# Two feed-forward blocks on one Trainium2 core: gate and up products over two token thirds as seven block products instead of eight

## The reference, cut to what matters

```python
def swiglu_ffn(x, g, w_gate, w_up, w_down):
    h = rmsnorm(x, g)
    return (jax.nn.silu(h @ w_gate) * (h @ w_up)) @ w_down

x = x + 0.5 * swiglu_ffn(x, lp['ffn1_norm'], ...)
...                                    # attention, gated DeltaNet, cross-attention
x = x + 0.5 * swiglu_ffn(x, lp['ffn2_norm'], ...)
```

## Time and profile before

| | us |
|---|---|
| median of 3 runs | 3365.69 |
| the profiled execution, time | 3355.45 |
| its span, first to last instruction | 3353.7 |
| PE busy | 3228.4 (96%) |
| DVE / ACT / POOL busy | 1323.4 / 676.0 / 958.2 (39% / 20% / 29%) |
| granted TensorE clock, mean | 0.993 of 2.4 GHz |
| first FFN: matmuls of turn 0 from | 99.33 |
| first FFN: end, about | 925 |
| second FFN: from / to, about | 2480 / 3340 |

### The profile page before, as it was taken

One profiled execution on the slowest core, in us unless ns is written; L12 is line 12 of the kernel. 1 busy time (PEld: TensorE's weight loads), 2 busy tenths in 40 slices (PEclk: granted clock), 3 DMA queues, 4 the chain that ended last, 5 costly groups with the idle time before them and its releaser, 6 DMA issues.

```text
span 3353.7 us, 50033 instructions
## 1 busy us (share of the span) xinstructions
PE 3228.4 (96%) x19961; PEld 3073.1 (92%) x19961; DVE 1323.4 (39%) x2297; ACT 676.0 (20%) x1318; POOL 958.2 (29%) x436
## 2 busy tenths in 40 slices
PE   6999999999999999999999999999899999999998
PEld 4999999999978888888888989988799999999997
DVE  3232233333356655653342465232334332333324
ACT  5100000000133333433433342133311000000001
POOL 4434333333322222211112133221133333333341
PEclk9999999999999999999999999999999999999999
DMA  5411111111142233211112145024311111111111
GB/s 185 137 38 44 44 44 44 40 41 44 42 164 75 95 129 136 78 41 69 58 50 83 40 163 177 20 100 160 126 44 45 45 38 43 44 44 38 38 44 63
DMA packets 92168, 247.36 MB, mean 74 GB/s; under 512 B 11536, under 2 KB 49168, under 8 KB 89360
## 3 DMA queue, kind: packets, MB, share of 16 engines
q1 hardware_dynamic: 48640, 154.09, 14.0%
q10 hardware_dynamic: 43408, 91.55, 7.5%
HBM read 197.87 MB, written 47.75 MB: 73 GB/s over the span
## 4 chain that ended last, share of the span: by engine, by line
PE 87%; DVE 6%; issue 2%; ACT 2%; POOL 1%; DMA 1%; ACTq 0%; DVEq 0%; POOLq 0%
PE psum L164 60%; PE psum L260 13%; PE psum L1797 1%; DVE n_tmp L557 1%; PE psum L1733 1%; PE psum L939 1%; PE psum L2767 1%; POOL w_lo L2272 1%; PE psum L1009 1%; PE psum L984 1%; PE psum L2740 1%; DVE a_sc L1334 1%; PE psum L1747 1%; PE psum L1741 1%; PE psum L2746 1%
## 5 line engine op out<-in xcount | busy, mean ns | idle before, releaser
L131 POOL TENSOR_TENSOR w_hi<-w_raw,zero 128x1024 fp32r<-128x1024 f32 x199 | 383.9, 1929 | 2096.4 <-PE psum L164 1312.3
L164 PE MATMUL psum<-x_hi,w_hi 128*128 128x384 f32 x2928 | 573.8, 336 | 16.2 <-DVE x_lo L574 4.1
L164 PE MATMUL psum<-x_lo,w_hi 128*128 128x384 f32 x2928 | 572.6, 335 | 0.0
L164 PE MATMUL psum<-x_hi,w_lo 128*128 128x384 f32 x2928 | 569.9, 334 | 0.0
L164 PEld LDWEIGHTS psum<-x_hi,w_hi 128*128 128x128 f32 x2928 | 512.2, 188 | 24.4 <-issue 12.5
L164 PEld LDWEIGHTS psum<-x_lo,w_hi 128*128 128x128 f32 x2928 | 514.4, 188 | 1.9
L164 PEld LDWEIGHTS psum<-x_hi,w_lo 128*128 128x128 f32 x2928 | 513.1, 188 | 0.0
L134 POOL TENSOR_TENSOR w_lo<-w_raw,w_hi 128x1024 fp32r<-128x1024 f32 x199 | 494.2, 2483 | 15.6
L419 DVE TENSOR_TENSOR f_hid<-psum,f_gate 128x384 f32<-128x384 f32 x132 | 73.6, 558 | 858.9 <-PE psum L164 856.5
L366 ACT ACTIVATE f_gate<-psum 128x384 f32<-128x384 f32 x132 | 64.8, 493 | 1478.3 <-PE psum L164 1474.6
L164 PE MATMUL psum<-f_h_hi,w_hi 128*128 128x384 f32 x1056 | 269.6, 336 | 0.0
(11 more groups left out here) (303 smaller groups left out, 3365.0 us busy)
## 6 DMA issues: line engine op xcount, KB each, us to landing
w_raw<-units SPq DMA_DIRECT2D x224, 512.0 KB, 3.6
gate_dram<-b_stash ACTq DMA_DIRECT2D x48, 192.0 KB, 1.9
e_gate<-gate_dram ACTq DMA_DIRECT2D x48, 192.0 KB, 2.9
a_kc<-k_cache ACTq DMA_DIRECT2D x4, 2048.0 KB, 7.7
a_vc<-v_cache ACTq DMA_DIRECT2D x4, 2048.0 KB, 12.2
proj_dram<-a_cv ACTq DMA_DIRECT2D x12, 576.0 KB, 2.7
b_pad<-proj_dram SPq DMA_DIRECT2D x12, 576.0 KB, 4.9
x_sk<-mem_k ACTq DMA_DIRECT2D x6, 1024.0 KB, 7.9
```

Source lines behind the costliest of these rows:

```text
L131: pool.tensor_tensor(k.w_hi[s][:, :], k.w_raw[s][:, :], k.zero[:, 0:1].to_broadcast([P, D]), ALU.add)\
L164: mm = pe.matmul(out, wl if part == 2 else wh, (xl if part == 1 else xh)[:, n0:n1], start=(part == 0 and i == 0), stop=(part == 2 and i == ...
```

## The change

In every turn but turn 0 of both FFNs, the gate products (pair 0) and then the up products (pair 1) of two hidden blocks and the first two token thirds are made as one 2 x 2 x 2 block product with seven block products instead of eight (Winograd's form). A is the weight matrix in four halves (output block x channels 0 to 511 or 512 to 1023), B the activations in four blocks (channel half x third 0 or 1). Four sums of weight halves (S1 to S4) and four sums of activation blocks (T1 to T4) are needed, and sums of the products afterwards. The last third stays whole. A pair is now 9 jobs: 7 of 12 matmuls and 2 of 24.

- The T blocks are made once per FFN, during turn 0, by 12 DVE instructions of 128 x 1536 and 4 ACT copies (`TokenSums`).
- The S halves are made by POOL in every turn: 4 sums of 128 x 512 per pair.
- Weights are split by halves, 20 a turn. The upper part is now made by ACT (Copy, `upper`), the remainder by POOL (`lower`).
- DVE keeps partial sums of products in SBUF (`keep`), finishes them (`add`), and for four of the six hidden blocks of a turn multiplies sum and gate, both in SBUF (`hidden_sum`).
- Pairs use PSUM banks 4 to 7, down jobs banks 0 to 3. The next turn's halves in slot 0 (A11, A12) are split when the 18 pair jobs of a turn are done.
- Turn 1 is written out on PE as well. Some buffers of the norms move in memory.

```diff
+ITEM_HALF = (0, 1, 4, 2, 3, 5, 2, 0, 1, 3, 4, 5, 2, 0, 5, 1, 3, 2, 4, 5)
+ITEM_AFTER = (-24, -24, -4, -4, 0, 0, 3, 4, 4, 5, 6, 8, 8, 9, 12, 13, 13, 14, 15, 17)
...
     def gpsimd(pool):
...
+        def lower(i, p, name):
+            m = item(p, name)
+            pool.wait_ge(k.unit_hi.sem, items(k.unit_hi, i, m))
...
+            pool.wait_ge(k.dense_done.sem, done(i, ITEM_AFTER[m - 1]))
+            h = ITEM_HALF[m - 1]
+            pool.tensor_tensor(half(k.w_lo, h), raw_of(p, name), half(k.w_hi, h).bitcast(F32), ALU.subtract)\
+                .then_inc(k.unit_split.sem, 1)
+        def total(i, p, out, in0, in1, op):
+            pool.tensor_tensor(raw_of(p, out), raw_of(p, in0), raw_of(p, in1), op).then_inc(k.w_summed.sem, 1)
+        def turn(i):
+            for p in range(2):
+                lower(i, p, "A11")
+                lower(i, p, "A12")
+                if p == 0:
+                    pool.wait_ge(k.h_ready.sem, k.h_ready.at(6 * i))
+                landed(i, p, "A21")
...
+                total(i, p, "S1", "A21", "A22", ALU.add)
+                total(i, p, "S3", "A11", "A21", ALU.subtract)
+                lower(i, p, "S1")
...
+                total(i, p, "S2", "A22", "S3", ALU.subtract)
...
+                total(i, p, "S4", "A12", "S2", ALU.subtract)
+                for m in ("S2", "S3", "A22", "A21", "S4"):
+                    lower(i, p, m)
+            for m in ("D0b", "D0a", "D1a", "D1b"):
+                lower(i, 2, m)
...
     def tensor(pe):
...
+        def pair(i, p):
...
+            block(i, p, 0, "A11", ts.b11)
...
+            block(i, p, 1, "A12", ts.b21)
+            split(i, p, "S2")
+            bank_free(2)
+            block(i, p, 2, "S2", ts.t2)
+            bank_free(3)
+            whole(i, p, 3, "A11", "A12")
+            split(i, p, "S3")
+            bank_free(4)
+            block(i, p, 4, "S3", ts.t3)
+            bank_free(5)
+            block(i, p, 5, "S1", ts.t1)
...
+            block(i, p, 6, "A22", ts.t4)
...
+            whole(i, p, 7, "A21", "A22")
...
+            block(i, p, 8, "S4", ts.b22)
...
     def scalar(act):
...
+        def upper(i, p, *names):
...
+                act.wait_ge(k.dense_done.sem, done(i, ITEM_AFTER[m - 1]))
+                act.activation(half(k.w_hi, ITEM_HALF[m - 1]), raw_of(p, name), ACT.Copy).then_inc(k.unit_hi.sem, 1)
...
     def vector(dve):
...
+        def hidden_sum(i, j, c, n, added, which, job):
...
+            add(i, 1, s, which, job)
...
+            dve.tensor_tensor(h_hi[:, c, third(n)], s, g, ALU.mult).then_inc(k.gate_used.sem, 1)
+            dve.tensor_tensor(s, s, g, ALU.mult).then_inc(k.hid_made.sem, 1)
+            lower(i, j, c, n)
...
+        def turn(i):
...
+            keep(i, 1, 4, 5)
+            hidden_sum(i, 3, 1, 0, 7, 3, 6)
+            hidden_bank(i, 4, 1, 2, 7)
+            hidden_sum(i, 5, 0, 1, 8, 4, 8)
+            add_down(i, False)
```

More of the change, by code:

```diff
@@ L71, in last_use, with load_units @@
     return (0, same[at - 1]) if at else (1, same[-1])
-def load_units(sp, k, first, turns, turn, at_turn=None, then=None, apart=0):
+def load_units(sp, k, first, turns, turn, at_turn=None, then=None, apart=0, last=True):
     def one(i, j):
@@ L111, in units_ahead, with split_units @@
     return min(RING, k.turn_sizes[k.phase + 1]) if k.phase + 1 < len(k.turn_sizes) else 0
-def split_units(pool, k, turns, jobs, first=None, left=None):
+def split_units(pool, k, turns, jobs, first=None, left=None, last=True):
     turn = len(jobs)
@@ L282, in ffn_phase @@
     by_unit = [(u, n) for u in range(4) for n in range(3)]
     by_third = [(u, n) for n in range(3) for u in range(3)] + by_unit[9:]
+    order = by_third if norm else by_unit
+    at = {un: g for g, un in enumerate(order)}
+    gates = [(u // 2, n) for u, n in order if u % 2 == 0]
+    turns = NFF // 2
     LAST = turns - 1
[L286 to L291, removed]
@@ L327, in turn, with block @@
                     norm.sums(pe, 2)
-                if memory and isinstance(i, int) and i == 0 and g == 0:
+                if memory and g == 0:
                     memory.turn_last(pe)
+        def block(i, p, job, name, xs):
+            h = ITEM_HALF[item(p, name) - 1]
+            wh, wl = half(k.w_hi, h), half(k.w_lo, h)
+            tiles = [(wh[:, c * P:(c + 1) * P], wl[:, c * P:(c + 1) * P], xs[0][:, c, :], xs[1][:, c, :]) for c in range(4)]
+            product(pe, k.ps[bank_of(p, job)][:, 0:THIRD], tiles, 0, THIRD).then_inc(k.dense_done.sem, 1)
@@ new lines, in whole, with split @@
+        def whole(i, p, job, lower, upper):
+            tiles = []
+            for c in range(KD):
+                h = ITEM_HALF[item(p, lower if c < 4 else upper) - 1]
+                cs = slice((c % 4) * P, (c % 4 + 1) * P)
+                tiles.append((half(k.w_hi, h)[:, cs], half(k.w_lo, h)[:, cs], xh[:, c, :], xl[:, c, :]))
+            product(pe, k.ps[bank_of(p, job)][:, 0:THIRD], tiles, 2 * THIRD, T).then_inc(k.dense_done.sem, 1)
+        def split(i, p, name):
+            pe.wait_ge(k.unit_split.sem, items(k.unit_split, i, item(p, name)))
@@ L384, in scalar @@
             bias_rows.store(act)
-        turn(0, gates_of(0)[2 if norm else 0:])
+        first_gates(gates[2 if norm else 0:])
+        for m in (1, 2, 3, 4):
+            ts.upper(act, m)
         with act.Fori(1, turns) as i:
```

386 lines of the change are left out of this document (327 added, 59 removed).

## The result

| | median us | lowest to highest | executions |
|---|---|---|---|
| before | 3365.3 | 3363.18 to 3367.87 | 4 |
| changed | 3318.3 | 3310.65 to 3321.29 | 4 |

The ratio is 0.9857, 95% interval 0.9838 to 0.9875: 47.0 us less. The forecast was 3311, with 3281 to 3342 as its range. The profiled execution of the changed kernel took 3310.65 us (span 3308.9, mean granted clock 0.991), against 3355.45 of the profiled one before: 44.8 less.

The account below looks back on a forecast made before the run. PE's matmuls were taken to bound the kernel. -83.2 (fewer matmuls) + 24.3 (stall) + 2.3 (last turn) + 2 (turn 0) = -54.6 us, so 3365.7 becomes 3311; range 3281 to 3342, to hold 8 in 10.

Parts of the forecast that it names:

- The price of the matmuls: FFN loop turns: 24 fewer matmuls at 0.1733 us each, a turn of 70.72 us, 83.2 us off the path in all.
- doesn't do what it says: Rival, PE's loop turns: restarts after waits at 42 jobs instead of 36 eat the saving; 3365 us, chance 0.03.
- POOL's half: POOL's 128 x 512 instructions in each loop turn: 1.3 us each, 28 of them 36 us a turn.
- The rival of halves near a whole (2.48): POOL's halves cost nearly a whole; slower from 1.93 us per piece with its gap, 3514 us at 2.5; chance 0.06.
- The stall: End of pair 1: DVE's two-SBUF instructions alternate with POOL, PE's fifth down job 1.35 us late; 18 turns, 24.3 us.
- The last turns: Last turn of each FFN: 2.3 us lost in the first, where POOL has a whole unit; 0 in the second.
- The weight chains: Loop turns: split weights and their sums reach PE in time, all hidden, so the split costs 0.
- chain (b): Pair 1: S2, needed at 27.04 us of the turn, is ready by 24.5; margin 2.5 us.
- chain (a): Start of a turn: S2, needed at 4.16 us, is ready at 2.2; margin 2.0 us.
- The rival of longer waits (3336): Later loads, POOL halves at 1.6 us or a late fourth remainder add 1 to 1.5 us a turn; chance 0.2.
- Turn 0: First turn of each FFN: 12 extra DVE instructions of 1.75 us each, mostly hidden; cost 1 us per FFN, bounds 0 to 5.
- The rival of the free end (3284.5): End of pair 1: the port lock falls out of the way, PE is fed throughout, only turn 0 costs; chance 0.2.

Follow-up runs that it names:

- e1: Changed kernel with POOL waiting for the sixth hidden block before making the next turn's first two remainders (or splitting the whole unit): 3288.21 us, ratio 0.9773.
- e2: Changed kernel with DVE adding the first two down products before it makes the sixth hidden block, POOL left as it was: 3287.56 us, ratio 0.9769.
- e4: Changed kernel with only A12, one of the next turn's two first POOL halves, made after DVE's last hidden block: 3294.32 us, measured once.
- e5: Changed kernel with one extra POOL sum (S1 made twice, same values) in each pair 1: 3315.49 us, measured once.
- e6: Changed kernel with three extra POOL sums (S1 again, same values) in each pair 1: 3369.42 us, measured once.
- e3: Changed kernel with the edits of e1 and e2, and token-sum steps 6 to 12 moved later in the second FFN's turn 0: 3283.37 us, ratio 0.9752.
- e7: As e3, with token-sum steps 8 to 12 placed one to two down adds earlier: 3282.65 us, ratio 0.9759.
- c2: The kernel before, unedited, profiled a second time: stretch between the FFNs 1481.02 us, against 1471.57 in its first profile.
- c1: The changed kernel, unedited, measured and profiled again: 3318.55 us, ratio 0.9863.

## Why the prediction was right, and where it was off

Times below are by the profiled executions, forecast against measured.

- **The price of the matmuls held.** A turn is 72.22 = 408 x 0.1733 + 1.50, and in e1 and e2, without the stall, 70.7. Nothing was lost in restarts at 42 jobs instead of 36: a loop turn has one gap, in its down part, and no other. The rival "doesn't do what it says" falls with this.
- **POOL's half held.** 1.29 us against 1.3 taken; L457's mean is 1327 ns with waits in it. With the figure of the Trainium skill's "GPSIMD Engine Reference", section 3.1 (4497 ns for 2048 columns), the prediction's estimate was 1.33; as an estimate, a straight line through that figure and the trace's 2.40 for 1024 gives 1.35, and the sum by it 3313 instead of 3312. The trace is near both, and its 1.29 decides. The rival of halves near a whole (2.48) falls, and its threshold (1.93 in the prediction, 1.95 by its own formula) is far.
- **The stall held in place, cause and size.** The wait comes at the fifth down job, ended by DVE's x add, 1.50 a turn against 1.35. Counted from the turn's first matmul at 248.01, L801 ends at 48.5, L802 at 50.1 and the first add at 51.3, where the prediction had 48.4, 50.1 and 51.25. The two in SBUF took 1.67 and 1.64. Shown by taking POOL's halves away in time (e1), by taking DVE's adds out from behind them (e2), and by halving it (e4). The page "SBUF — State Buffer" of the Trainium skill (section "SBUF: two separate sides") says that a DVE instruction with two SBUF inputs and a GpSimd instruction lock a shared pair of ports against each other, whichever starts first, for its whole length. The trace agrees: those that meet a POOL instruction wait for its end (1.67 and 1.64 us instead of 0.56), those that read PSUM do not (551 and 558 ns). The missing 0.15 is the restart of 0.11 and 0.04 in the rounding of the ends, over 18 turns 2.7 us.
- **The last turns held.** First FFN 2.6 against 2.3 (an idle of 2.31 and the restart), second 0 against 0.
- **The weight chains held.** No wait of PE on POOL in an FFN's loop turns. For chain (b), e5 shows that 1.4 us more are hidden, e6 that 4.1 are not; the margins of chain (a) and of the last halves were not tried, and only the missing waits speak for them. The rival of longer waits (3336) needed one of these margins used up, and none was; a load landed in 3.8 us, 0.2 over the figure taken.
- **Turn 0 was mis-sized.** The forecast was 1 us in each FFN. It was 0 in the first and 3.5 in the second, in two gaps (PE's timeline of the changed kernel):

```profile
2545.37 0.61 PE L168 MATMUL psum<-f_h_hi,w_hi 128*128 128x384 f32 x2 [1.41 <-DVE f_h_hi L729]
2548.17 0.62 PE L168 MATMUL psum<-f_h_hi,w_hi 128*128 128x384 f32 x2 [1.49 <-DVE x_late L760]
```

  The step that failed was "1.75 us each", and with it "Nine lie between hidden blocks 4.16 us or more apart, where PE's banks are already read": the fourth down job waits for L729, which reads the sixth block's bank, and the fifth for the first add. DVE's timeline of that turn 0:

```profile
2526.68 3.94 DVE L338 TENSOR_TENSOR f_q<-x_hi,x_lo 128x1536 f32<-128x1536 f32 x1
2530.66 3.33 DVE L341 TENSOR_TENSOR f_q<-f_q,f_q 128x1536 f32<-128x1536 f32 x1
2533.91 3.95 DVE L344 TENSOR_TENSOR f_q<-f_q,f_q 128x1536 f32<-128x1536 f32 x1
...
2539.37 1.75 DVE L347 TENSOR_TENSOR f_r<-f_q,f_r 128x1536 fp32r<-128x1536 f32 x1
```

  POOL was splitting whole units there (its timeline):

```profile
2528.96 3.41 POOL L133 TENSOR_TENSOR w_hi<-w_raw,zero 128x1024 fp32r<-128x1024 f32 x1
2532.45 3.80 POOL L136 TENSOR_TENSOR w_lo<-w_raw,w_hi 128x1024 fp32r<-128x1024 f32 x1
```

  It is the same taking of turns as in the stall, with larger pieces on both sides: these three are steps with both inputs in SBUF, 11.2 us where three free ones are 5.3, and POOL's two take 3.41 and 3.80 where free ones are 1.89 and 2.40. I had priced the lock at the stall and left it out for these nine steps. In the first FFN the steps stand elsewhere and only two of them meet POOL (3.95 and 3.45 us); its fourth hidden block begins 8.1 us before the down part, in the second FFN 2.9 us before it. So the first has the time that the second lacks. e3 and e7 move the steps, and both gaps go.

**The sum by stretches**, forecast against the difference of the two profiles. First FFN: -41.6 + 12.2 + 2.3 + 1 = -26.1; measured -28.0, which is -41.6 + 9 x 1.50 + 2.6, and -2.6 more because the kernel before had a wait in its own turn 0 (2.31 at 118.81, for ACT) that this profile of the changed one lacks; over the profiles of the changed kernel and its edits that wait comes and goes (2.25 or 2.26 in six, 0.16 and 0.26 in two, none in this one). No term of the forecast had it: that the two FFNs come out within 2.2 us of the forecast together is in part luck. Second FFN: -41.6 + 12.2 + 1 = -28.4; measured -24.5, which is -41.6 + 13.5 + 3.5. Together -54.6 against -52.4. The stages around the FFNs: 0 against +7.6, of which 6.5 lie in the stretch between them. By c2 that stretch is as long in the kernel before at another time, so it isn't the change's: the first profile of before was short there. All of it sums to the measured -44.8. By medians it was -47.0. Of the 7.3 us between 3311 and 3318.3, then, with the wait in the first FFN's turn 0 taken as equal on both sides, 1.5 are turn 0, 2.7 + 0.3 the restarts behind the waits, and 2.8 stay open: they are within what the stretch between the FFNs varies by (10.5 us), but nothing here shows that this is where they lie. The low end of the prediction's own range, 3300, does not come out of its terms: POOL at 1.19 and turn 0 at 0 give 3305. Nothing rests on it.

The rival of the free end (3284.5) described what e1 and e2 are, 3288.21 and 3287.56: the lock falls out of the way if POOL's halves come later, or DVE's adds sooner. The code did neither.

## What to carry to other kernels

Before you move arithmetic from PSUM to SBUF on DVE, look at what POOL has released by the same event: each DVE instruction with two SBUF inputs can have to wait for one POOL instruction (1.1 us here, for one of 1.29), and the price is paid wherever DVE's result feeds the bottleneck soonest. Price it in every stage where the two meet, prologue turns too. One wait placed on POOL's side (or two adds pulled ahead on DVE's) brought 30 us of 3318 with no work removed. And measure hidden margins by adding work: 1.4 us more of POOL cost nothing (e5), 4.1 us more cost the whole gain (e6).

## What the runs showed of the hardware

- A wait of PE costs more than the idle time that the profile shows: 1.22 shown was 1.50 from start to start.
- PE's waits on POOL in e6 (1.35 to 1.98 us) were followed in 8 of 20 cases by a stretch at a granted clock of 0.50 (1.2 GHz), which made a turn 1.5 us longer than a like one without it. The wait of 1.49 in turn 0 of the second FFN was followed by one in e1, e2, e4 and e6, and not in the changed kernel, c1 or e5; the wait of 2.31 in the first FFN of the kernel before was not in its first profile and was in c2. Equal waits, then, came out either way. After the gaps of 1.22 to 1.32 us before the fifth down job it was never seen (0.58 to 0.62 us for the pair behind, 72 gaps of the changed kernel, c1, e5 and e6).
- Beside each other, a DVE instruction with two SBUF inputs and a POOL instruction each waited for the other's end: 1.67 us instead of 0.56 on DVE (128 x 384), 2.85 instead of 2.54 for two on POOL (128 x 512); with larger pieces 3.3 to 3.95 instead of 1.75 on DVE, 3.41 and 3.80 instead of 1.89 and 2.40 on POOL.
- POOL's tensor_tensor on 128 x 512 took 1.29 us against 2.40 for 128 x 1024, so cutting one in two costs 0.18 us. ACT's copy of 128 x 512 into w_hi took 0.63.
